# Sums of squares of nine norms: four blocks added on VectorE, four multiplications with ones in place of eight

## The chip, the cores and the metric

The kernel runs on one core of one Trainium2 chip. The metric is the device time of one execution in microseconds (us), the median of several runs. A core has four engines that compute, each with an instruction queue of its own worked off in order: TensorE (PE in the profile; PEld is its loading of weights), VectorE (DVE), ScalarE (ACT) and GpSimd (POOL). The queue of SyncE (SP) issues the DMAs. Engines wait for one another by semaphores.

## The reference

Two transformer-like blocks of two layers each, all in float32, on 256 tokens of width 1024. The first block has a gated recurrence, an mLSTM and an attention to a memory in each layer, merged, projected and added to the stream x, then a dense feed-forward (layer 0) or eight experts (layer 1). The second block has two streams, x and a context, with differential, neighbourhood and windowed attention and feed-forwards modulated by a condition vector. Ahead of each part stands a root-mean-square norm over the 1024 values of a token:

```python
def rms_norm(x, g):
    xf = x.astype(jnp.float32)
    y = xf * lax.rsqrt(jnp.mean(xf * xf, axis=-1, keepdims=True) + EPS)
    return (y * g.astype(jnp.float32)).astype(x.dtype)

        x = x + merged @ w_out[l]
        h2 = rms_norm(x, norm_ffn_g[l])
        ...
        x = x + f
    return rms_norm(x, final_norm_g)
```

The change concerns the norms whose input is just being made by a projection with a residual, as `h2` here.

## The kernel before

**Layout.** The stream x lies transposed in SBUF, as eight blocks of 128 features by 256 tokens. A product in float32 is made from three products of rounded halves: each weight tile (128 x 2048 values, 1 MB, in one of three slots) is copied to its high half by ScalarE (line 1855, WH) and its low half is subtracted by VectorE (line 2244, WL); TensorE then does high by high, high by low and low by high for each of the blocks summed over (lines 1534 to 1536). A projection of eight 128-row blocks takes 24 matmuls for each output block of 128 features; a weight tile serves two output blocks. The last slices of the feed-forwards have fewer rows to sum over: 18 matmuls a block in g0c, g0x and g1 (tiles of 128 x 1536).

**The residual and the norm.** When TensorE has an output block in PSUM, VectorE adds it to x (line 2395 in the first part, line 2421, scaled, in the second; `kout`, by pairs of blocks, for x1.1). ScalarE squares the new block of x into a scratch (line 1874, `nsq`). The sum over the features runs across partitions, so TensorE makes it: a 128x128 matrix of ones times each of the eight blocks of squares, accumulated in one PSUM bank (line 1564, `nsum`). Then VectorE scales the mean (line 2295), ScalarE takes the inverse root (line 1880), VectorE refines it (lines 2268 to 2270) and applies it (line 2319), and the halves of the result are made for the next projection (lines 1897, 1902, 2327, 2330).

**The order.** The program is a list of units, written out by a planner that runs when the kernel is built (`Plan`). `put` appends a unit and moves the planner's clock by the cost of TensorE's part; the costs of the other engines are in `work`. Each engine then goes through the list and issues its part of each unit, so an engine's order is that of the list. Chains of attention and the like are threaded between the units of a projection (`weave`) when the clock has passed the time at which their next step is due. A weight tile is split ahead: unit `tile` stands in front of a pair of output blocks, and its split is that of the tile three later in the list.

**The nine norms.** `follow(name)` gives the function that is called behind each output block i of a projection: it appends the squaring of block i and, from i = 1 on, the sum of block i-1; behind block 7 also that of block 7. It serves f0 and f1 (behind `wo`), x1 (behind the last products of `ffn`), c0.1 and x0.1 (behind `wab0` and `wab1`), c1.0, x1.0 and final2 (behind the last slices of `g0c`, `g0x`, `g1`) and x1.1 (behind `wc`, whose pairs of blocks end only in the last quarter of its matmuls). The other norms (x0, mem0, mem1, c0.0, final1, x0.0) are summed in other ways. The bank of the sums is taken with the first sum and held until `root`, the unit `nmid`.

Of the kernel before, what the change touches and what calls it, by code (L numbers as in the profile page):

```python
# [10 lines left out]
F32 = mybir.dt.float32  # L11
# [4 lines left out]
T = 256  # L16
# [224 lines left out]
def work(p, unit):  # L241
# [37 lines left out]
    if kind == "napp":  # L279
        if len(args) > 1:  # L280
            return ((V, 0.85),) if args[1] < 4 else ((A, 0.6), (V, 0.65))
        if p.norms[args[0]]["dst"] is None:
            return ((V, 3.2),)
        return ((V, 6.4), (A, 0.4), (V, 0.8)) if "gn" in p.norms[args[0]] else ((V, 5.2), (A, 0.55), (V, 0.7))
    if kind == "nsq":
        return ((A, 0.33 * (args[2] - args[1])),)
# [10 lines left out]
class Plan:  # L297
# [190 lines left out]
    def follow(self, name):  # L488

        def after(i):  # L490
            self.squares(name, i, i + 1)
            if i:
                self.sums(name, i - 1, i)
            if i == 7:
                self.sums(name, 7, 8)
        return after
# [976 lines left out]
def tensor_program(nc, T_, pe, plan, mem, v):  # L1473
# [92 lines left out]

    def ada(l, q):
# [27 lines left out]
    def s(name, qb, m):  # L1595
# [6 lines left out]
        if spec["bias"]:  # L1602
            pe.wait_ge("band_r")
            if spec["kind"] == "near":
                tile = plan.tile["bias", spec["hd"]]
                pe.wait_ge(f"land{tile.slot}", tile.turn)
                b = tile.raw[:, 0, qb * T:qb * T + T]
            else:
                b = mem["BAND"][:, 128 + qb * T:128 + qb * T + T]
            eight = mem["BAND"][:, 0:128]  # L1610
            last = T_.matmul(ps[:, 256:512], eight.bitcast(F32) if spec["kind"] == "near" else eight, b, start=False, stop=True)
# [208 lines left out]
    do = {"lin": lin, "kout": kout, "nsum": nsum, "ada": ada, "turned": turned, "s": s, "t": t, "v": vv, "sub1": sub1, "rope1": rope1, "if": iff, "acol": acol,  # L1820
# [406 lines left out]
def vector_program(nc, V, dv, plan, mem, v):  # L2227
# [63 lines left out]

    def nmid(name):
        m, y, u = (R[:, i, :] for i in range(3))
        dv.wait_ge("ps", "norm", name, 8)
        V.tensor_scalar(m, bank(("norm", name))[:, 0:T], 1.0 / D, EPS, mult, add).then_inc(*dv.done("norm_m", name))
        dv.frees("norm", name)
        dv.wait_ge("norm_s", name)
        rstd(m, y, u)
# [461 lines left out]
    do = {"start": start, "lam": lam, "tile": tile, "lin": lin, "nmid": nmid, "napp": napp, "cvd": cvd, "turned": turned, "e": e,  # L2760
# [270 lines left out]
```

## Time and profile before

| | |
|---|---|
| median of 3 runs | 3476.21 us (3470.22 to 3481.88) |
| profiled execution | 3476.61 us, span of the trace 3474.8 us |
| TensorE matmuls busy | 3299.8 us, 95% |
| VectorE busy | 2332.3 us, 67% |
| ScalarE busy | 1838.8 us, 53% |
| granted clock of TensorE, mean | 0.971 of full |
| chain that ended last | TensorE 77%, VectorE 12%, ScalarE 8% |

The profile shows one execution. Times are microseconds from the start of the span, durations of groups are means. In a timeline or chain a row is one or several equal instructions: start, duration, engine, line of the kernel, operation, what it writes and reads, their number (x2), and in square brackets how long the engine was idle before it and which engine and line ended that. Matmuls are pipelined and the ends shown are modelled, so the distance between starts is what a matmul costs. `CTX` in the rows of the first part is a scratch of the norm, which shares its place with the context of the second part. The chain of waits is followed back from the last instruction.

### The profile page before, as it was taken

The numbers are of one execution on the slowest core, as the hardware profiler recorded it, in microseconds if no ns is written. First come the engines' busy times: TensorE is split into PE (matmuls) and PEld (weight loads), VectorE is DVE, ScalarE is ACT, GpSimd is POOL, SyncE is SP. The second block draws the span as 40 slices with busy tenths as digits, with TensorE's granted clock in tenths as the row PEclk, the third lists the DMA queues.
The fourth block names the chain that finished last, engine by engine and source line by source line (L and its number), as shares of the span: only waits on it lengthen the run. The fifth ranks groups of instructions, "written<-read, shape, count | busy, mean of one in ns | idle before, by whom it ended". The sixth has DMA issues, their size and how long they took to land.

```text
span 3474.8 us, 56477 instructions
## 1 busy us (share of the span) xinstructions
PE 3299.8 (95%) x24379; PEld 3047.0 (88%) x24379; DVE 2332.3 (67%) x2986; ACT 1838.8 (53%) x2194; POOL 0.2 (0%) x4
## 2 busy tenths in 40 slices
PE   8999999999899899999999999899799999999798
PEld 7988999999889799999999999888587889985698
DVE  6876655578766588888888888745565556465454
ACT  5464544454635377777777777633443444335343
POOL 0000000000000000000000000000000000000000
PEclk9999999999999899999999999999799999999899
DMA  6432565454325599899899899611233456530353
GB/s 249 170 134 97 182 231 194 158 194 146 134 97 184 214 373 351 327 355 350 333 351 352 334 352 344 252 68 61 109 111 134 141 222 233 211 127 13 134 191 112
DMA packets 102815, 723.43 MB, mean 208 GB/s; under 512 B 11680, under 2 KB 13344, under 8 KB 16672
## 3 DMA queue, kind: packets, MB, share of 16 engines
q1 hardware_dynamic: 102560, 719.73, 56.3%
q8 instruction: 196, 3.21, 0.4%
q14 instruction: 59, 0.48, 0.0%
HBM read 718.64 MB, written 1.05 MB: 207 GB/s over the span
## 4 chain that ended last, share of the span: by engine, by line
PE 77%; DVE 12%; ACT 8%; issue 2%; DMA 1%; SPq 0%; DVEq 0%; ACTq 0%
PE PS L1534 13%; PE PS L1535 13%; PE PS L1536 13%; PE PS L1487 6%; PE PS L1485 6%; PE PS L1486 6%; DVE WL L2244 4%; ACT WH L1855 3%; PE PS L1793 3%; PE PS L1791 3%; PE PS L1792 3%; PE PS L1632 2%; PE PS L1601 2%; PE PS L1564 1%; PE PS L1577 1%
## 5 line engine op out<-in xcount | busy, mean ns | idle before, releaser
L2244 DVE TENSOR_TENSOR WL<-RAW,WH 128x2048 fp32r<-128x2048 f32 (+2 forms) x428 | 963.0, 2252 | 578.0 <-ACT WH L1855 572.4
L1855 ACT ACTIVATE WH<-RAW 128x2048 fp32r<-128x2048 f32 (+2 forms) x428 | 802.6, 1878 | 252.7 <-PE PS L1536 183.6
L1534 PE MATMUL PS<-PH,WH 128*128 128x256 f32 x2464 | 710.8, 288 | 39.2 <-DVE PL L2440 7.9
L1536 PE MATMUL PS<-PH,WL 128*128 128x256 f32 x2464 | 697.2, 283 | 0.0
L1535 PE MATMUL PS<-PL,WH 128*128 128x256 f32 x2464 | 697.2, 283 | 0.0
L2244 DVE TENSOR_TENSOR WL<-F,WH 128x2048 fp32r<-128x2048 f32 x210 | 481.2, 2292 | 87.4 <-ACT WH L1855 86.4
L1534 PE MATMUL PS<-HPH,WH 128*128 128x256 f32 (+1 forms) x1648 | 496.7, 301 | 24.6 <-DVE HPL L2330 12.6
L1534 PEld LDWEIGHTS PS<-PH,WH 128*128 128x128 f32 x2464 | 471.2, 191 | 47.9 <-issue 29.2
L1535 PE MATMUL PS<-HPL,WH 128*128 128x256 f32 (+1 forms) x1648 | 481.2, 292 | 0.0
L1536 PE MATMUL PS<-HPH,WL 128*128 128x256 f32 (+1 forms) x1648 | 480.8, 292 | 0.0
L1535 PEld LDWEIGHTS PS<-PL,WH 128*128 128x128 f32 x2464 | 471.1, 191 | 1.3
L1536 PEld LDWEIGHTS PS<-PH,WL 128*128 128x128 f32 x2464 | 471.0, 191 | 0.0
L1855 ACT ACTIVATE WH<-F 128x2048 fp32r<-128x2048 f32 x210 | 402.3, 1916 | 77.8 <-PE PS L1793 48.4
L1485 PE MATMUL PS<-WH,PH 128*128 128x256 f32 x1456 | 420.1, 289 | 2.0 <-ACT PL L2117 1.0
L1486 PE MATMUL PS<-WL,PH 128*128 128x256 f32 x1456 | 410.4, 282 | 0.0
L1487 PE MATMUL PS<-WH,PL 128*128 128x256 f32 x1344 | 379.8, 283 | 0.0
L1534 PEld LDWEIGHTS PS<-HPH,WH 128*128 128x128 f32 x1648 | 318.5, 193 | 42.1 <-issue 23.6
L1535 PEld LDWEIGHTS PS<-HPL,WH 128*128 128x128 f32 x1648 | 319.2, 194 | 4.7
L1536 PEld LDWEIGHTS PS<-HPH,WL 128*128 128x128 f32 x1648 | 318.4, 193 | 4.5
L1485 PEld LDWEIGHTS PS<-WH,PH 128*128 128x128 f32 x1456 | 274.3, 188 | 5.3 <-ACT WH L1855 1.2
L1486 PEld LDWEIGHTS PS<-WL,PH 128*128 128x128 f32 x1456 | 275.8, 189 | 3.0
L1487 PEld LDWEIGHTS PS<-WH,PL 128*128 128x128 f32 x1344 | 253.6, 189 | 0.0
(382 smaller groups left out, 5072.8 us busy)
## 6 DMA issues: line engine op xcount, KB each, us to landing
F<-in_moe_w SPq DMA_DIRECT2D x210, 1024.0 KB, 5.5
RAW<-in_ffn_w SPq DMA_DIRECT2D x130, 1024.0 KB, 4.9
RAW<-in_moe_w SPq DMA_DIRECT2D x126, 1024.0 KB, 5.1
RAW<-in_w_in SPq DMA_DIRECT2D x64, 1024.0 KB, 4.9
F<-in_ada_w SPq DMA_DIRECT2D x18, 1024.0 KB, 11.5
RAW<-in_w_kv SPq DMA_DIRECT2D x16, 1024.0 KB, 4.9
G<-in_ada_w SPq DMA_DIRECT2D x15, 1024.0 KB, 10.4
RAW<-in_w_in_ab SPq DMA_DIRECT2D x12, 1024.0 KB, 5.0
```

Of the source, the lines that this page charges most:

```text
L1485: T_.matmul(out, lh, rh, start=i == 0, stop=False)
L1486: T_.matmul(out, lh, rl, start=False, stop=False)
L1487: last = T_.matmul(out, ll, rh, start=False, stop=i == n - 1)
L1534: T_.matmul(out, lh, rh, start=first, stop=False)
L1535: T_.matmul(out, lh, rl, start=False, stop=False)
L1536: last = T_.matmul(out, ll, rh, start=False, stop=end)
L1601: last = T_.matmul(ps, l, r, start=i == 0, stop=i == len(ops) - 1 and not spec["bias"])
L1791: T_.matmul(out, oh[:, c], wh, start=j == 0 and k == 0, stop=False)
L1792: T_.matmul(out, oh[:, c], wl, start=False, stop=False)
L1793: last = T_.matmul(out, ol[:, c], wh, start=False, stop=j == 13 and k == 1)
L1855: S.activation(mem["WH"][:, t.s % NHL, 0:m], v.raws[t.slot][:, 0:m], ACT.Copy).then_inc(*ac.done("w_hi", t.s))
L2244: V.tensor_tensor(mem["WL"][:, t.s % NHL, 0:m], v.raws[t.slot][:, 0:m], mem["WH"][:, t.s % NHL, 0:m].bitcast(F32), sub).then_inc(*dv.done( ...
```

## The change

Four of the eight sums of squares of each of the nine norms go to VectorE. `follow` still appends the squaring of block i behind block i. Behind blocks 2 to 5 it appends a new unit `nadd` for block i-1: VectorE waits for the square of that block and adds it to the square of block 0, in place. The units `nsum` in mid-projection are gone. Behind block 7, a bank is taken and one unit `nsum2` is appended, with a cost of 1.72 us in the planner: TensorE waits for the four adds and multiplies the added block 0 with ones, then blocks 5, 6 and 7, each with its wait for the square, into one bank. `nadd` costs 0.35 us of VectorE in the planner. In `s` the two cases of the bias matmul are written out apart.

```diff
--- before.py
+++ after.py
@@ -282,6 +282,8 @@
         if p.norms[args[0]]["dst"] is None:
             return ((V, 3.2),)
         return ((V, 6.4), (A, 0.4), (V, 0.8)) if "gn" in p.norms[args[0]] else ((V, 5.2), (A, 0.55), (V, 0.7))
+    if kind == "nadd":
+        return ((V, 0.35),)
     if kind == "nsq":
         return ((A, 0.33 * (args[2] - args[1])),)
     return OTHER.get(kind, ())
@@ -489,10 +491,11 @@
 
         def after(i):
             self.squares(name, i, i + 1)
-            if i:
-                self.sums(name, i - 1, i)
+            if 1 < i < 6:
+                self.put("nadd", name, i - 1)
             if i == 7:
-                self.sums(name, 7, 8)
+                self.bank(("norm", name), self.bgc, True)
+                self.put("nsum2", name, cost=1.72)
         return after
 
     def modulation(self, n, slots=None, after=()):
@@ -1564,6 +1567,16 @@
             last = T_.matmul(PS[:, plan.banks.place["norm", name], 0:T], ones, v.blocks(tmp, k, k + 1)[:, 0, :], start=k == 0, stop=k == 7)
         last.then_inc(*pe.done("ps", "norm", name, k1))
 
+    def nsum2(name):
+        tmp, out = scratch_of(plan, name), bank(("norm", name))[:, 0:T]
+        consts()
+        pe.wait_ge("added", name, 4)
+        T_.matmul(out, ones, v.blocks(tmp, 0, 1)[:, 0, :], start=True, stop=False)
+        for k in (5, 6, 7):
+            pe.wait_ge("sq", name, k)
+            last = T_.matmul(out, ones, v.blocks(tmp, k, k + 1)[:, 0, :], start=False, stop=k == 7)
+        last.then_inc(*pe.done("ps", "norm", name, 8))
+
     def ada(l, q):
 
         c, b = mem["C32"], plan.banks.place["ada", l, q]
@@ -1601,14 +1614,12 @@
             last = T_.matmul(ps, l, r, start=i == 0, stop=i == len(ops) - 1 and not spec["bias"])
         if spec["bias"]:
             pe.wait_ge("band_r")
-            if spec["kind"] == "near":
-                tile = plan.tile["bias", spec["hd"]]
-                pe.wait_ge(f"land{tile.slot}", tile.turn)
-                b = tile.raw[:, 0, qb * T:qb * T + T]
-            else:
-                b = mem["BAND"][:, 128 + qb * T:128 + qb * T + T]
-            eight = mem["BAND"][:, 0:128]
-            last = T_.matmul(ps[:, 256:512], eight.bitcast(F32) if spec["kind"] == "near" else eight, b, start=False, stop=True)
+        if spec["kind"] == "near" and spec["bias"]:
+            tile = plan.tile["bias", spec["hd"]]
+            pe.wait_ge(f"land{tile.slot}", tile.turn)
+            last = T_.matmul(ps[:, 256:512], mem["BAND"][:, 0:128].bitcast(F32), tile.raw[:, 0, qb * T:qb * T + T], start=False, stop=True)
+        elif spec["bias"]:
+            last = T_.matmul(ps[:, 256:512], mem["BAND"][:, 0:128], mem["BAND"][:, 128 + qb * T:128 + qb * T + T], start=False, stop=True)
         last.then_inc(*pe.done("ps", "s", name, qb, m))
 
     def t(name, qb):
@@ -1817,7 +1828,7 @@
             pe.wait_point("region_end", ("act", "dve"))
         pe.leave(had)
         plan.swap()
-    do = {"lin": lin, "kout": kout, "nsum": nsum, "ada": ada, "turned": turned, "s": s, "t": t, "v": vv, "sub1": sub1, "rope1": rope1, "if": iff, "acol": acol,
+    do = {"lin": lin, "kout": kout, "nsum": nsum, "nsum2": nsum2, "ada": ada, "turned": turned, "s": s, "t": t, "v": vv, "sub1": sub1, "rope1": rope1, "if": iff, "acol": acol,
           "ml": ml, "router": router, "rtop": rtop, "slots": slots, "tt": tt, "gather": gather, "up": up, "turn": turn, "down": down,
           "finish": finish, "region": region}
     for kind, *args in plan.units:
@@ -2288,6 +2299,14 @@
         dv.turn(V.tensor_scalar(e, lam, -1.0, 0.0, mult, mx))
         dv.turn(V.tensor_tensor(q, q, e, add))
         V.tensor_scalar(mem["LAMS"][:, :], q, -2.0, None, mult).then_inc(*dv.done("lam"))
+
+    def nadd(name, k):
+        tmp = scratch_of(plan, name)
+        total = v.blocks(tmp, 0, 1)[:, 0, :]
+        dv.wait_ge("sq", name, k)
+        if k > 1:
+            dv.wait_ge("added", name, k - 1)
+        V.tensor_tensor(total, total, v.blocks(tmp, k, k + 1)[:, 0, :], add).then_inc(*dv.done("added", name, k))
 
     def nmid(name):
         m, y, u = (R[:, i, :] for i in range(3))
@@ -2757,7 +2776,7 @@
             last = V.scalar_tensor_tensor(mem["GN"][:, l, i, s_, :], mem["MOD"][:, l, s_, (3 * i + 1) * 8:(3 * i + 2) * 8], 1.0,
                                               P(f"norm_g2_{l}{i}", 0, 8), add, mult)
         last.then_inc(*dv.done("gains", l, i))
-    do = {"start": start, "lam": lam, "tile": tile, "lin": lin, "nmid": nmid, "napp": napp, "cvd": cvd, "turned": turned, "e": e,
+    do = {"start": start, "lam": lam, "tile": tile, "lin": lin, "nadd": nadd, "nmid": nmid, "napp": napp, "cvd": cvd, "turned": turned, "e": e,
           "n": n, "sub2": sub2, "rope2": rope2, "rgc": rgc, "row": row, "acol": acol, "ml": ml, "pair": pair, "yml": yml, "mgd": mgd, "h2d": h2d, "kout": kout,
           "router": router, "rtop": rtop, "slots": slots, "ttl": ttl, "sel": sel, "gather": gather, "up": up, "turn": turn, "leave": leave, "finish": finish,
           "region": region, "second": second, "lam2": lam2, "gains": gains}
```

## Rows read from the trace of the kernel before

**Rows 1.** The page, busy time by engine.

```profile
PE 3299.8 (95%) x24379; PEld 3047.0 (88%) x24379; DVE 2332.3 (67%) x2986; ACT 1838.8 (53%) x2194; POOL 0.2 (0%) x4
```

**Rows 2.** Waits of TensorE: us in total, times, longest us.

```profile
PE PS L1564 <- ACT G L1874: 15.9, 15, 3.0
PE PS L1564 <- ACT CTX L1874: 11.5, 7, 7.9
```

**Rows 3.** Timeline of TensorE, end of final2: start us, us, instruction, count, idle before it.

```profile
3459.68 0.28 PE L1536 MATMUL PS<-HDH,WL 128*128 128x256 f32 x1
...
3460.35 0.28 PE L1535 MATMUL PS<-HDL,WH 128*128 128x256 f32 x1
...
3462.39 0.59 PE L1564 MATMUL PS<-G,CST 128*128 128x256 f32 x2
3463.58 0.70 PE L1564 MATMUL PS<-G,CST 128*128 128x256 f32 x2 [0.60 <-ACT G L1874]
```

**Rows 4.** Timeline of VectorE, end of final2.

```profile
3462.59 0.48 DVE L2421 SCALAR_TENSOR_TENSOR X<-PS,MOD,X 128x256 f32<-128x256 f32 x1 [2.10 <-PE PS L1536]
...
3465.28 0.43 DVE L2268 TENSOR_TENSOR R<-R 128x256 f32<-128x256 f32 x1 [0.55 <-ACT R L1880]
```

**Rows 5.** Timeline of TensorE, first sum of f0.

```profile
448.09 0.67 PE L1564 MATMUL PS<-CTX,CST 128*128 128x256 f32 x2 [0.76 <-ACT CTX L1874]
```

**Rows 6.** Timeline of VectorE, residuals 5 and 7 of f0.

```profile
461.51 0.42 DVE L2395 TENSOR_TENSOR X<-X,PS 128x256 f32<-128x256 f32 x1 [1.23 <-PE PS L1536]
...
468.07 0.42 DVE L2395 TENSOR_TENSOR X<-X,PS 128x256 f32<-128x256 f32 x1 [1.22 <-PE PS L1536]
```

**Rows 7.** Chain of work in c1.0, start us, us, what.

```profile
2789.53 1.91 ACT WH L1855
2791.46 2.29 DVE WL L2244
2793.75 0.41 DVE CTX L2421
2794.18 0.43 ACT G L1874
2794.65 0.70 PE PS L1564 x2
```

**Rows 8.** Timeline of TensorE, sum 6 of x1 and of x0.1.

```profile
724.59 1.13 PE L1564 MATMUL PS<-CTX,CST 128*128 128x256 f32 x4 [0.63 <-ACT CTX L1874]
...
2823.13 1.13 PE L1564 MATMUL PS<-G,CST 128*128 128x256 f32 x4 [1.64 <-ACT G L1874]
```

**Rows 9.** Timeline of VectorE, tail of x0.1 and first residuals of x1.1.

```profile
2817.74 4.49 DVE L2244 TENSOR_TENSOR WL<-RAW,WH 128x2048 fp32r<-128x2048 f32 x2 [2.29 <-ACT WH L1855]
...
3239.65 0.87 DVE L2421 SCALAR_TENSOR_TENSOR X<-PS,MOD,X 128x256 f32<-128x256 f32 x2
```

**Rows 10.** Busy time by stretch: TensorE, its weight loads, VectorE, ScalarE, GpSimd, clock, DMA.

```profile
2489.80:2493.00 3.20, 0.25 (x3) 0.11 (x2) 3.17 (x5) 0.42 (x1) 0.00 (x0) 1.00 0.11 13
2493.20:2497.80 4.60, 4.60 (x27) 4.56 (x26) 2.73 (x8) 1.69 (x2) 0.00 (x0) 0.63 0.53 214
```

**Rows 11.** Chain of work behind the sums of x1.1.

```profile
3252.54 3.59 PE PS L1577 x64
```

**Rows 12.** DMA issues from 3215 to 3262 us: size, median us to landing.

```profile
RAW<-in_ada_w SPq DMA_DIRECT2D x2, 1024.0 KB, 8.8
```

**Rows 13.** Chain of work over the span, the same two places in each layer.

```profile
225.81 7.17 PE PS L1632 x32
...
442.93 1.91 ACT WH L1855
...
916.72 7.17 PE PS L1632 x32
...
1135.43 1.91 ACT WH L1855
```

**Rows 14.** Busy time of an attention stretch, columns as in rows 10.

```profile
2505.00:2777.00 272.00, 252.54 (x1735) 218.60 (x1733) 151.68 (x254) 116.81 (x176) 0.00 (x0) 0.96 0.33 121
```

## The prediction

> **What bounds the kernel now.** I read the shares of the engines first, then the list of TensorE's waits, then the timelines and chains of the nine places that the change touches. TensorE's matmuls fill 95% of the span [rows 1], so work taken from TensorE comes off the time wherever nothing else is late. The sums of the norms (line 1564) are among the longest waits: TensorE stood 15.9 and 11.5 us in front of them for ScalarE's squares, 7.9 us of that once at the start of the program, outside the change [rows 2]. So there are two things to gain, the sums' own matmuls and waits in front of those in mid-projection, and one question: what ends each projection once the sums are gone. That is read from VectorE and ScalarE, which in the same microseconds split the weights of the next tiles, add the residual and square it, in program order.
>
> **What a sum costs.** A sum is two passes of the array (x2). At the end of final2, the last norm, the matmul ahead of a sum starts at 3459.68 and the second matmul behind it at 3460.35 [rows 3]; from there to the next sum at 3462.39 are 17 matmuls, 0.12 us each. 0.67 less two steps of 0.12 is **0.43 us** a sum, with TensorE never idle. In all nine norms that are summed as their projection goes (f0, x1, f1, c0.1, c1.0, x0.1, x1.0, x1.1, final2) sum k stands behind block k+1, so six sums (0 to 5) stand ahead of the end of block 7, the last of the projection: 6 x 0.43 = 2.6 us.
>
> **What the new tail costs.** After block 7 the kernel before does sum 6, waits for the square of block 7 and does sum 7: 3462.39 to 3463.58 from the start of one to that of the other [rows 3], 1.19 us. The new tail has three matmuls there (the added blocks 0 to 4, block 5, block 6), 3 x 0.43 = 1.29 us, so sum 7 starts 0.1 us later. What covers them is the residual, 0.48 [rows 4], the square, 0.43 [rows 7], and the steps between; without that cover they would cost 0.86 us each time.
>
> **What the adds cost.** Four tensor-tensor adds of 128x256 on VectorE for each norm, 36 in all. The nearest row is the same operation and shape at line 2268, 0.43 us [rows 4]; a residual add counts 0.41 to the next start [rows 7]. Each add waits for a square that is a block old. Behind it in VectorE's order stand the next residual, the low half of the next weight tile and, in c0.1, steps of softmax; for those TensorE waits later. Where VectorE idles (1.23 us before the residual at 461.51 [rows 6]) the add is free. Between the residuals of the two blocks that follow a weight split it isn't: there it lies on the loop below. Bounds: 0 and 36 x 0.41 = 14.8 us; I take what each place gives.
>
> **The loop that takes over.** For each pair of blocks ScalarE squares the second block (0.43), copies the high half of a weight tile (1.91), VectorE subtracts for the low half (2.29), and only then adds the residuals of the next two blocks, whose squares follow [rows 7]. Start to start that is 0.43 + 1.93 + 2.29 + 0.43 = 5.1 us, and 0.41 for the second residual: 5.5 before, up to 5.9 with an add between the residuals. TensorE's side is two blocks of 24 matmuls, 6.56 us with two sums (461.51 to 468.07 [rows 6]), 5.7 without; in c1.0 and x1.0, whose projections end with blocks of 18 matmuls, 36 x 0.12 = 4.3 us. So:
>
> - f0 and f1: 5.7 against 5.5 to 5.9, level. Six sums 2.6, plus the wait of 0.76 in front of sum 0 [rows 5], less 0.25 for an add between residuals 4 and 5 and for the tail: **3.1 each, 6.2**.
> - final2 has no more weights to split: 2.6 - 0.1 = **2.5**.
> - x0.1: two tiles are split together behind block 5 (4.49 us) [rows 9], and TensorE already waits 1.64 us in front of sum 6 [rows 8]. Only sums 0 to 3 stand ahead of block 5's end: 4 x 0.43 = **1.7**.
> - x1: it waits 0.63 us in front of sum 6 [rows 8], and VectorE also makes halves of another norm in each block. The loop rules from block 2: sum 0 and a wait of 0.4 in front of it, **0.8**.
> - c1.0 and x1.0: the loop rules already. For c1.0: high half 2789.53, low half 2791.46, residual 2793.75, sum 2794.65 [rows 7]. What is saved before block 3 (two sums and a wait of 0.7, 1.6 us) shrinks to 0.7 at the next split, since residual 3 comes behind residual 2, a half of another product and an add, and to 0.2 at the last, behind one add more: **0.2**; x1.0, without the other product's halves, **0.5**. TensorE ends block 7 some 4 us (c1.0) and 3 us (x1.0) before the last square.
> - c0.1: softmax of attention heads runs between its blocks. The wait of 2.95 us in front of sum 4 (2489.8 to 2493.0, TensorE busy 0.25 of 3.20) goes [rows 10], but VectorE has that softmax behind its weight split, and residuals 5 to 7 move by less than a microsecond: **0.9**; bounds -1 (the adds in front of softmax) and 5.5 (2.6 + 2.95).
> - x1.1: its squares start in the last quarter of its matmuls, 12 a pair of blocks, 1.4 us, and TensorE has idled by then for the residual at 3239.65 [rows 9]; the sums end at 3252.54 [rows 11]. After: VectorE has 0.8 for residuals and 0.8 for adds a pair, so the first pair of residuals ends at 3240.5, the last at 3240.5 + 3 x 0.8 + 4 x 0.4, or 3244.6 with a step of waiting; squares 3245.1, sums 3245.9. That is 6.6; 1.7 goes back to the clock (below): **4.9**. The matmuls behind (line 1577) need two loads that took 8.8 us each [rows 12], the last about when it is wanted; bound -2 if it is late.
>
> Sum: 6.2 + 2.5 + 1.7 + 0.8 + 0.2 + 0.5 + 0.9 + 4.9 = 17.7 us.
>
> **The clock.** Behind the 2.95 us wait the granted clock was 0.63 over 4.60 us [rows 10]: 0.37 x 4.60 = 1.7 us of work lost, part of it at 1.2 GHz instead of 2.4. The new waits in the tails of c1.0 (4 us) and x1.0 (3 us) are as long or longer, so I take 1.7 us each, +3.4; the bounds are 0 and twice that. The Trainium skill (TensorE: Matmul & The Clock Gate, section Loop structure matters more than you think) says that VectorE's work on results between tiles leaves the array warm and that a long wait for a DMA cools it. The row at 2493.2 speaks against that, since no DMA was waited for. By the page the sum would keep its 17.7.
>
> **The order.** The planner in the program counts 1.72 us for the sums at a norm's end where it counted 3.44, and holds a PSUM bank for a shorter time, so its later choices (between which blocks a softmax step is put) may differ. I cost that at nothing, since the engines' totals hardly change, with a bound either side: the same stretch of layer 0 (225.81 to 442.93) and of layer 1 (916.72 to 1135.43), 217.1 and 218.7 us, differ by 1.6 us [rows 13]. Some nine such stretches follow f0 outside the experts' part: 1.6 x 3 = 5 us either way. The experts' part only starts earlier. Lines 1601 to 1611 are rewritten to the same matmuls: nothing.
>
> **Result.** 17.7 - 3.4 = 14.3 us off. The profiled execution took 3476.61 us around a span of 3474.8; 3476.61 - 14.3 = 3462.3, and the median of the runs, 3476.21, lies 0.4 us from it: **3462 us**, -0.4%.
>
> **The rivals.**
> - TensorE bound everywhere: six sums go in nine places (23.2), all waits in front of sums in mid-projection (7.1 of the 19.5 that rows 2 leave, the largest 2.95 [rows 10] and 0.76 twice [rows 5]), 4 more in x1.1 and 1.7 of clock in c0.1: 36.0, 3441 us. For it: 95%. Against: the loop of rows 7 and the waits of rows 8.
> - The clock holds through the tails: 17.7, 3459 us. Against: rows 10; for: those tails may fall otherwise in time. The page above says the same.
> - More clock and a worse order: the tails of x1 and x0.1 (2 us idle) fall to half clock too, 3.4, and order takes 5: 3471 us. For it: their waits come near those that cost the clock.
> - The sums don't come off the path, or the adds eat what they free: 3476 us. Against: 0.67 against 0.24 in rows 3.
> - Slower: in the attention stretches, where softmax is threaded between blocks, TensorE already idles, 272 - 252.5 = 19.5 us in one of them [rows 14]. If the new order puts a weight split (1.91 + 2.29 = 4.2 us [rows 7]) ahead of a softmax step that TensorE waits for, each such place costs 4.2 us. From six of them on (25 us against 14.3 + 10.4) the kernel is slower by more than 0.3%; seven give 3492 us. Against: the two layers' 1.6 us.
>
> **How the numbers follow.** Forecast 0.42, clock holds 0.13, TensorE bound 0.12, clock and order 0.23, no effect 0.04, slower 0.06. About 0.3% (10.4 us) is what a measurement of this kernel can tell from no change. Faster by more: 0.42 + 0.13 + 0.12, less 0.04 for the edge of the forecast: 0.63. Within: 0.04 + 0.23 + 0.04 = 0.31. Slower: 0.06. The range reaches from near the TensorE-bound case, as far as c0.1's bound (4.6 more), order (5) and the clock (3.4) carry it together with 3 of the runs' spread, to past the clock-and-order case: 3446 to 3474.
>
> **What would show it.** 36 adds of 0.4 us on VectorE at the new line; 72 passes in place of 144 for these norms. TensorE's idle time in front of the last sums: 3 to 4 us in c1.0 and x1.0, under 0.3 in f0, f1 and final2. The stretch from x1.1's last quarter to line 1577 shorter by 5 to 7 us. Half clock just behind c1.0 and x1.0. The prediction is wrong if the tails of c1.0 and x1.0 show no wait (then 3441 is near), or if the attention stretches change by more than 5 us.

## The result, and the profile after

The changed kernel takes 3435.8 us (median, 3432.9 to 3442.3), the kernel before 3473.2 us in the same runs: a ratio of 0.9893, 95% interval 0.9871 to 0.9914. That is 37 us off, where 14 were forecast, and below the forecast range of 3446 to 3474 us. The profiled execution took 3434.04 us around a span of 3432.3. One execution of the run e8 below took 10974.8 us at a mean granted clock of 0.283 and is left out of its median.

The page of the changed kernel: busy time by engine. It answers to [rows 1]: 72 matmuls fewer, 36 instructions more on VectorE.

```profile
PE 3272.1 (95%) x24307; PEld 3027.7 (88%) x24307; DVE 2342.6 (68%) x3022; ACT 1844.5 (54%) x2198; POOL 0.2 (0%) x4
```

TensorE's waits in the changed kernel (us in total, times, longest), and one of the two groups of adds from the list of groups (count, us busy, mean ns, idle before). They answer to [rows 2]. Line 1567 is the other norms' sums, which the change doesn't touch. Of the 27.4 us of [rows 2] the waits that began before 7.88, 2237.07 and 2261.10 us (7.88, 1.93 and 0.92 us) stood in front of those other norms. So the nine norms' waits go from 16.7 to 10.1 + 2.4 + 1.8 = 14.3 us: fewer, and now at the ends.

```profile
PE PS L1577 <- ACT G L1885: 10.1, 5, 3.7
...
PE PS L1567 <- ACT CTX L1885: 7.8, 1, 7.8
...
PE PS L1577 <- ACT CTX L1885: 2.4, 1, 2.4
PE PS L1567 <- ACT G L1885: 2.1, 1, 2.1
PE PS L1574 <- DVE G L2309: 1.8, 1, 1.8
...
L2309 DVE TENSOR_TENSOR G<-G 128x256 f32<-128x256 f32 x24 | 10.0, 417 | 0.2
```

The tails in the changed kernel, from the timeline of TensorE (start us, us, instruction, count, idle before): line 1574 multiplies the added block, 1577 blocks 5 to 7. In this order f0, x1, c1.0 (three rows), x0.1, x1.0, x1.1, final2.

```profile
465.46 1.03 PE L1577 MATMUL PS<-CTX,CST 128*128 128x256 f32 x4
...
720.19 1.13 PE L1577 MATMUL PS<-CTX,CST 128*128 128x256 f32 x4 [2.39 <-ACT CTX L1885]
...
2760.60 0.59 PE L1574 MATMUL PS<-G,CST 128*128 128x256 f32 x2
2761.03 0.59 PE L1577 MATMUL PS<-G,CST 128*128 128x256 f32 x2
2765.36 2.07 PE L1577 MATMUL PS<-G,CST 128*128 128x256 f32 x4 [3.73 <-ACT G L1885]
...
2794.18 1.13 PE L1577 MATMUL PS<-G,CST 128*128 128x256 f32 x4 [1.64 <-ACT G L1885]
...
3014.22 1.13 PE L1577 MATMUL PS<-G,CST 128*128 128x256 f32 x4 [2.92 <-ACT G L1885]
...
3210.36 0.72 PE L1574 MATMUL PS<-G,CST 128*128 128x256 f32 x2 [1.80 <-DVE G L2309]
...
3419.83 0.59 PE L1574 MATMUL PS<-G,CST 128*128 128x256 f32 x2
```

No idle time at f0 and final2, 3.7 us at c1.0, 2.9 at x1.0: these are the tails that the prediction described.

**Where the 42.5 us between the two spans lie.** The medians differ by 37.4 us, the two profiled executions by 5 us more. The same work must stand between two cuts. ScalarE copies 638 weight tiles to their high halves in both kernels, in the same order (line 1855 before, 1866 after), so I cut each trace at the starts of these splits, counted from 0:

| splits | what lies there | before us | after us | change |
|---|---|---|---|---|
| 60 to 64 | f0 | 34.18 | 30.36 | -3.8 |
| 100 to 113 | x1 | 67.80 | 67.06 | -0.7 |
| 166 to 169 | f1 | 34.19 | 30.60 | -3.6 |
| 519 to 546 | c0.1 and the heads of differential and neighbourhood attention | 263.18 | 243.81 | -19.4 |
| 546 to 562 | c1.0, x0.1 | 122.67 | 122.08 | -0.6 |
| 562 to 595 | g0x, x1.0 | 190.95 | 190.27 | -0.7 |
| 595 to 604 | windowed attention | 172.30 | 168.91 | -3.4 |
| 604 to 609 | x1.1 | 70.48 | 64.33 | -6.2 |
| 637 to the end | final2 | 27.08 | 24.20 | -2.9 |

The rest of the span gives 1.3 us. One row stands out: 19.4 us in a stretch for which I had 0.9 and "nothing, 5 us either way". Busy time in that stretch, before and after (columns as in rows 10):

```profile
2469.53:2732.71 263.18, 237.82 (x1549) 200.51 (x1548) 147.23 (x263) 113.50 (x179) 0.00 (x0) 0.94 0.32 116
```

```profile
2460.03:2703.84 243.81, 229.19 (x1539) 193.76 (x1538) 148.20 (x267) 118.46 (x183) 0.00 (x0) 0.97 0.35 126
```

TensorE's idle time falls from 25.4 to 14.6 us. Its busy time falls by 8.6 us. Eight matmuls of c0.1's sums are gone, 8 x 0.21 = 1.7 us; the rest is the clock, 0.94 before and 0.97 after.

The planner's lists of units show what else changed. Every unit but sums and adds stands in the same order in both kernels, except between split 520 and the middle of the stretch. There the steps of two attention heads, which went in pairs, go one by one. In the lists below s is a head's scores, e its maximum and exponential, n its scaling, t its transposes, v its product with the values, sub0 to sub2 its own norm; nmid and napp are root and application of c0.1; `...` marks what is left out.

```
before:  t d1.0 0, t d1.1 0 | wab0 block 3, first half | s d1.0 1, s d1.1 1 | second half ...
after:   t d1.0 0 | wab0 block 3, first half | s d1.0 1, t d1.1 0 | second half | e d1.0 1, s d1.1 1 ...

before, behind block 7:  gains, v d1.0, v d1.1, nmid, sub0 d1.0, sub0 d1.1, sub1 d1.0, sub1 d1.1,
                         sub2 d1.0, s d1.2 0, sub2 d1.1, e d1.2 0, s d1.3 0, napp
after, behind block 7:   v d1.0, gains, t d1.1 1, sub0 d1.0, nmid, v d1.1, sub1 d1.0, sub0 d1.1,
                         sub2 d1.0, s d1.2 0, sub1 d1.1, e d1.2 0, napp, sub2 d1.1, s d1.3 0
```

### The profile page after: what moved, and what is told of

Its sections match the earlier page's. It is cut to its first block, busy times and chain, and to the rows that moved or that the text cites. A ratio compares the mean times of both kernels' runs of the same rounds, so it can differ in the third digit from the quotient of the medians.

```text
span 3432.3 us, 56399 instructions
## 1 busy us (share of the span) xinstructions
PE 3272.1 (95%) x24307; PEld 3027.7 (88%) x24307; DVE 2342.6 (68%) x3022; ACT 1844.5 (54%) x2198; POOL 0.2 (0%) x4
## 4 chain that ended last, share of the span: by engine, by line
PE 76%; DVE 12%; ACT 8%; issue 2%; DMA 2%; SPq 0%; DVEq 0%; ACTq 0%
PE PS L1537 13%; PE PS L1539 13%; PE PS L1538 13%; PE PS L1490 6%; PE PS L1488 6%; PE PS L1489 6%; DVE WL L2255 4%; ACT WH L1866 4%; PE PS L1804 3%; PE PS L1802 3%; PE PS L1803 3%; PE PS L1643 2%; PE PS L1614 2%; PE PS L1631 1%; PE PS L1788 1%
```

## The experiments

All have the changed kernel's sums and adds unless said otherwise, and their edits are shown against it. "Old order" is that of the kernel before, "new order" that of the changed kernel. Medians of each run beside those of the kernel before in the same runs:

| run | median us | before us | ratio, 95% interval | splits 519 to 546, us |
|---|---|---|---|---|
| changed kernel | 3435.8 | 3473.2 | 0.9893 (0.9871 to 0.9914) | 243.8 |
| e1 new sums, old order | 3451.4 | 3471.0 | 0.9947 (0.9930 to 0.9963) | 259.3 |
| e5 old sums, new order | 3460.4 | 3473.2 | 0.9966 (0.9954 to 0.9979) | 246.2 |
| e3 third order | 3440.8 | 3471.0 | 0.9916 (0.9900 to 0.9933) | 250.9 |
| e7 other order behind c0.1 | 3449.0 | 3474.2 | 0.9931 (0.9915 to 0.9948) | 256.2 |
| e8 old order behind c0.1's sums | 3440.9 | 3474.2 | 0.9907 (0.9887 to 0.9926) | 250.2 |
| e11 old order, root first | 3451.8 | 3472.7 | 0.9942 (0.9926 to 0.9959) | 258.0 |
| e12 new order, root first | 3430.3 | 3472.7 | 0.9886 (0.9868 to 0.9904) | 241.1 |
| e9 every add twice | 3435.7 | 3474.2 | 0.9894 (0.9878 to 0.9911) | 245.9 |
| e10 eight sums at the end | 3440.8 | 3474.2 | 0.9910 (0.9893 to 0.9927) | 246.7 |
| e6 c1.0's tail moved | 3437.5 | 3473.2 | 0.9896 (0.9876 to 0.9916) | 244.8 |
| e4 five tails moved | 3425.4 | 3471.0 | 0.9867 (0.9850 to 0.9883) | 243.7 |
| e13 root and three tails | 3426.3 | 3472.7 | 0.9872 (0.9853 to 0.9892) | 243.1 |

**e1: the sums without the order.**

```diff
             if i:
+                if i == 1:
+                    self.bank(("norm", name), self.bgc, True)
+                self.clock += 0.43
             if 1 < i < 6:
-                self.put("nadd", name, i - 1)
+                self.units.append(("nadd", name, i - 1))
             if i == 7:
-                self.bank(("norm", name), self.bgc, True)
-                self.put("nsum2", name, cost=1.72)
+                self.clock += 0.43
+                self.units.append(("nsum2", name))
```

> The new sums and adds are issued where the changed kernel issues them, but the planner books their time and their PSUM bank as before, so every other unit of the program stands in the order of the kernel before. Theory A (the part missing from my sum comes from the attention steps' order behind c0.1): only the terms of the norms remain, as the two traces show them, f0 3.8, x1 1.1, f1 3.5, x0.1 1.8, x1.0 0.7, x1.1 5.7, final2 2.8, less 1.7 of clock behind c1.0, 17.7 us, and up to 3 for c0.1: 3452 to 3456 us beside 3473, and the stretch from 2505 to 2777 keeps its 272 us. Theory B (the sums and waits that left c0.1 and TensorE do it all, the order is worth nothing): 3436 us, as the changed kernel.

3451.4 us, 19.5 below the kernel before, half a microsecond under theory A's range; the stretch 519 to 546 took 259.3 us. Theory A, then. The sums by themselves are worth 19.5 us where 14.3 were forecast (17.7 less 3.4 of clock), and c0.1's part of that is 263.2 - 259.3 = 3.9 at most. That part isn't a wait that went: TensorE's idle time in the stretch is 27.4 us in e1 and was 25.4; its busy time is 6.0 us shorter, 1.7 of it the sums' own passes and the rest the clock, 0.96 for 0.94.

**e5: the order without the sums.** The eight multiplications stand where they stood; a bank is held in the place of the new one and the planner's clock is moved as in the changed kernel. The edit is shown against the kernel before; the lines that give the stand-in bank back and take it out of TensorE's waits are left out. A first version without the latter lines, e2, gave no result.

```diff
             if i:
-                self.sums(name, i - 1, i)
+                if i == 1:
+                    self.bank(("norm", name), self.fgc, True)
+                self.units.append(("nsum", name, i - 1, i))
+            if 1 < i < 6:
+                self.busy[V] += 0.35
             if i == 7:
-                self.sums(name, 7, 8)
+                self.units.append(("nsum", name, 7, 8))
+                self.bank(("spare", name), self.bgc, True)
+                self.clock += 1.72
```

> Eight multiplications with ones for each norm in their old places, no adds, but the planner books time and bank as in the changed kernel, so that all other units stand in its order. The new sums in the old order took 3451.4 us beside 3471.0 (-19.5). Theory A: the rest of the changed kernel's 37 us comes from the order of the attention steps and is found here alone: 3451 to 3457 us, and the stretch behind c0.1 is shorter by some 13 us. Theory B: the two only work together (the freed time in c0.1 lets the heads go ahead): 3465 to 3473 us.

3460.4 us, 12.8 below before: a smaller gain than theory A expected and a larger one than theory B. The stretch settles it: busy time from split 519 to 546 in this run,

```profile
2471.70:2717.86 246.16, 230.85 (x1549) 194.84 (x1548) 147.17 (x263) 118.35 (x183) 0.00 (x0) 0.97 0.34 124
```

The same 1549 matmuls as before take 17.0 us less: 10.1 us less idle (15.3 for 25.4), and 7.0 us less busy, which with equal matmuls is the clock. Sums alone give -3.9 in this stretch, order alone -17.0, both -19.4: they nearly add up. By the medians the two runs give 19.5 + 12.8 = 32.3 of the 37.4 us, which the intervals of the three ratios allow. Outside the stretch this trace of e5 was 2.2 us behind the kernel before at split 519, though the units ahead of it stand in the same order, and lost 2.6 in the windowed attention (below). Only c0.1's booking matters: written out with the old booking in one norm at a time, the planner's list changes for c0.1 and for no other.

**What the order changes at c0.1's end.** TensorE's waits from split 519 to 546 in e1, then in the changed kernel (us in total, times, longest):

```profile
PE PS L1541 <- DVE HPL L2353: 5.5, 1, 5.5
PE PS L1655 <- ACT TMP L2027: 3.4, 3, 2.6
PE PS L1581 <- ACT G L1889: 3.4, 2, 2.8
PE PS L1541 <- DVE HPL L2433: 3.1, 2, 1.9
```

```profile
PE PS L1614 <- ACT PQ L1999: 3.6, 2, 2.7
...
PE PS L1614 <- ACT PQ L2010: 1.9, 1, 1.9
PE PS L1577 <- ACT G L1885: 1.8, 2, 1.3
PE PS L1537 <- DVE HPL L2349: 1.3, 1, 1.3
```

The timeline of TensorE in e1 behind the sum (1581), and that of ScalarE:

```profile
2494.26 1.22 PE L1581 MATMUL PS<-G,CST 128*128 128x256 f32 x2 [0.58 <-ACT G L1889]
2495.28 4.82 PE L1647 MATMUL PS<-PQ,G 128*128 128x256 f32 x16
2502.70 1.10 PE L1655 MATMUL PS<-TMP,CST 128*128 128x256 f32 x4 [2.60 <-ACT TMP L2027]
...
2513.49 0.55 PE L1541 MATMUL PS<-HPH,WH 128*128 128x256 f32 x1 [5.54 <-DVE HPL L2353]
```

```profile
2498.41 0.38 ACT L2020 ACTIVATE G<-PS 128x256 f32<-128x256 f32 x1 [4.20 <-PE PS L1647]
2500.14 0.38 ACT L2020 ACTIVATE G<-PS 128x256 f32<-128x256 f32 x1 [1.34 <-PE PS L1647]
2500.54 1.28 ACT L1895 ACT_TABLE_LOAD   x1
2501.83 0.42 ACT L1895 ACTIVATE R<-R 128x256 f32<-128x256 f32 x1
```

Both heads have their product with the values at once (16 matmuls of line 1647), then both wait at once for their own norms on ScalarE and VectorE, the root of c0.1 stands behind both, and TensorE runs out of work twice, 2.60 and 5.54 us. In the new order one head still has transposes and its product to do while the other's norm is worked on. From the last sum to the first matmul of g0ca0 it is 2494.26 to 2513.49, 19.2 us, in e1, and in the changed kernel 2487.20 to 2502.96, 15.8 us. The Trainium skill (PSUM — Partial Sum Buffer, section Engine vs sequencer instructions) says that the queues of ScalarE and VectorE are strictly first in, first out. The rows agree: the root's input was ready at 2495.9, and its table load began at 2500.54, behind a copy that waited 4.20 us.

**e11 and e12: is it the root's place?** One unit moved, in the old order and in the new.

```diff
+        self.units.remove(("nmid", "c0.1"))
+        self.units.insert(self.units.index(("nsum2", "c0.1")) + 1, ("nmid", "c0.1"))
         self.units = splits_ahead(self.units, self.tiles, self.tile)
```

> The run with the sums alone (old order, 3451.4 us), with one unit moved: the root of c0.1 (scaling by VectorE, root by ScalarE, refinement by VectorE) stands directly behind its sum instead of behind the last products of the two heads. In that run the scaling was done at 2495.9 and ScalarE took the root at 2501.8, behind two copies that waited for 16 matmuls of the heads; TensorE then stood 5.5 us for the applied norm. Theory G (the order of the head steps is worth its 12 us because the norm's steps queue between them on ScalarE and VectorE): the table load of 1.3 us and the refinement of 1.4 us leave that queue, about 3 us less in the stretch 519 to 526, 3448 us. Rival (the heads' own steps rule, the norm follows them in any case): no change of that stretch of 83.7 us beyond 0.5.

> The changed kernel with the same unit moved. There the scaling ended at 2488.8, the root was taken at 2494.0 behind one product of the heads, and TensorE stood 2.65 and 1.27 us ahead of g0ca0. Theory G: 2 to 3 us less in the stretch of 70.8 us, 3433 us. Rival: 70.8 within 0.5, 3436 us.

In the old order splits 519 to 526 took 82.4 us for 83.7, and the wait of 5.5 us in front of g0ca0 was still there: 5.53. In the new order they took 68.1 for 70.8, and the median was 3430.3; the intervals of these two runs and of the runs without the move overlap, so the stretches carry this. So the root's place is worth 1.3 and 2.6 us, as part of the cause, but with the root moved in both, the two orders still differ by 258.0 - 241.1 = 16.9 us from split 519 to 546. Theory G holds for the new order and falls short in the old one. That the rest comes from two heads waiting at the same time is what the rows above suggest; no run shows it by itself.

**e3, e7, e8: other orders.** e3 books the bank with block 1 and the time with block 7. e7 adds the first line below, e8 the second:

```diff
     p.apply("c0.1")
     p.gap(3.0)
+    p.clock += 1.72
```

```diff
+    p.clock += -3
     p.lin_all(wab0, p.follow("c0.1"))
```

> The changed kernel's sums and adds, but the bank of the sums is booked with block 1 and the time with block 7, which gives a third order of the attention steps. Theory A (order moves the time by tens of us and has nothing to do with the sums): somewhere between 3436 and 3460 us, not at 3436, with the difference inside 2455 to 2680. Theory B: 3436 within 3 us.

> The changed kernel's sums, adds and order up to the place where the norm c0.1 is applied; 1.72 us are booked back there, so that the attention steps behind it fall into yet another order. In the runs so far the changed kernel's order gained 12 us from the first split of wab0's last tiles to the second split of the g0c part and 5 us in the hundred behind. Theory D (the gain comes from how many head steps are left to feed TensorE while c0.1 is summed, rooted and applied): the first 12 us stay and only the part behind moves, 3432 to 3446 us. Rival (each order is a lottery over the whole stretch): 3446 to 3460 us, the first part changed too.

> The changed kernel's sums and adds with the planner's clock set back 3 us ahead of c0.1's projection: its first blocks come in another order, everything from block 3 on stands in the order of the kernel before. Theory D: the waits at c0.1's end come back as in the run with the sums alone, 3449 to 3455 us. Rival (what counts is where the projection's first blocks stand): 3436 to 3445 us.

e8's expectation misdescribes its edit. By the planner's list the head steps go one by one from block 2 of wab0 to block 7, in places of their own, and only from the gains behind c0.1's last square on does the list stand in the old order. The run took 76.1 us for splits 519 to 526 where e1 took 83.7, and had the waits at c0.1's end as expected (2.60 and 5.35 us): with the heads out of step in the projection's blocks and in pairs behind them, 7.6 us are gained. By its median of 3440.9 us it falls into the rival's range. Theory D was right on the waits and wrong to put the whole gain there. The changed kernel's 70.8 us up to split 526 can't be set beside these two, since more of the heads' work stands behind that split there (371 matmuls ahead of it, 400 in e1, 394 in e8); of its gain on e1, 9.2 us are idle time of TensorE (10.3 for 19.5).

e3, 250.9 us in the stretch, shows that going one by one isn't enough. There too the heads' steps are apart, further than in the changed kernel: the product of the first head stands in block 7, and c0.1's root behind the product of the second. TensorE waits 5.36 and 5.64 us, and is idle 16.6 us from split 519 to 526:

```profile
2502.13 1.19 PE L1652 MATMUL PS<-TMP,CST 128*128 128x256 f32 x2 [5.36 <-ACT TMP L2024]
...
2514.01 2.07 PE L1615 MATMUL PS<-G 64*128 64x512 f32 x2 [5.64 <-ACT PQ L2011]
```

e7 kept the first part, whose units stand in the changed kernel's order (71.9 us, the changed kernel 70.8), but lost 11 us behind it: 256.2 us, and 3449.0. There my slower rival stands in the trace. Waits of TensorE from 2534 to 2719 us in e7, and ScalarE and VectorE ahead of the first of them:

```profile
PE PS L1632 <- DVE PQ L2492: 17.3, 2, 9.3
```

```profile
2594.47 1.91 ACT L1867 ACTIVATE WH<-RAW 128x2048 fp32r<-128x2048 f32 x1 [10.71 <-DMA RAW<-in_ffn_w]
2599.53 0.69 ACT L2000 ACTIVATE PQ<-PS,SM 128x512 f32<-128x512 f32 x1 [3.15 <-DVE SM L2479]
```

```profile
2596.41 2.29 DVE L2256 TENSOR_TENSOR WL<-RAW,WH 128x2048 fp32r<-128x2048 f32 x1 [11.24 <-ACT WH L1867]
2598.62 0.68 DVE L2475 TENSOR_REDUCE SM<-PS 128x1 f32<-128x512 f32 x1
```

A weight split stands ahead of the softmax steps of a head on both engines, the tile's load lands late, and both engines idle 11 us, while TensorE waits 9.33 us for what its transposes read (and 7.93 us in a second place, for the same line of VectorE). I had priced that place at the split's own 4.2 us; with a late load ahead of it, it cost twice that.

Five orders of the same units with the new sums (e1, e7, e3, e8, the changed kernel) thus took 259.3, 256.2, 250.9, 250.2 and 243.8 us in this stretch: the old order is the slowest of them, the changed kernel's the fastest.

**e9 and e10: the adds and the passes by themselves.** e9 adds a second addition behind each of the 36; e10 has no adds, and TensorE multiplies all eight blocks behind block 7; the planner books the same time as in the changed kernel.

```diff
         V.tensor_tensor(total, total, v.blocks(tmp, k, k + 1)[:, 0, :], add).then_inc(*dv.done("added", name, k))
+        again = v.blocks(tmp, k, k + 1)[:, 0, :]
+        V.tensor_tensor(again, again, again, add).then_inc(*dv.done("again", name, k))
```

```diff
-        pe.wait_ge("added", name, 4)
-        T_.matmul(out, ones, v.blocks(tmp, 0, 1)[:, 0, :], start=True, stop=False)
-        for k in (5, 6, 7):
+        for k in range(8):
```

> The changed kernel with a second addition of the same shape behind each of the 36 (its result is used nowhere): 36 x 0.41 = 14.8 us more on VectorE. Theory E (an add is on the path only in x1.1, 4 x 0.41 = 1.6, and between residuals where a weight split rules, 0.4 in some places): 1 to 5 us more, 3437 to 3441 us. Rival (VectorE is on the path at every add): 12 us more, 3448 us.

> The changed kernel without adds: TensorE multiplies all eight blocks of squares with ones behind block 7, in the changed kernel's order. Four passes of 0.43 us more at each of nine ends, 15.5 us of TensorE. Theory F (where TensorE waits for the last square anyway, c1.0, x1.0, x1, x0.1, they cost nothing; at f0, f1, final2, x1.1 they cost 1.7 each, less the adds that leave VectorE, 1.6 in x1.1 and 0.3 in f0 and f1): 4 to 6 us more, 3440 to 3442 us. Rival (all of it is on the path): 3451 us.

e9: 3435.7 us, the changed kernel's own time, with VectorE busy 2354.5 us for 2342.6. The adds cost nothing that the median can show, not even in x1.1 (splits 604 to 609: 64.6 us for 64.3). They aren't free everywhere: in c1.0 and x1.0, where VectorE is on the path, the last waits grow from 3.73 to 3.95 and from 2.92 to 3.59 us, and splits 546 to 557 take 63.1 us for 62.4. e10: 3440.8, 5 us more as theory F had it, though the intervals of the two kernels overlap. The stretches show the sum of it: f0 32.3 us for 30.4, f1 32.3 for 30.6, final2 25.7 for 24.2, and less than the changed kernel in c1.0 (61.7 for 62.4) and x1.0 (189.0 for 190.3). There the extra passes fill the wait (idle time from split 562 to 595: 0.8 us for 3.2) and the granted clock stayed at 1.00 behind both.

**e6, e4, e13: the tails.** Each moves the four multiplications behind work that doesn't need the norm; shown are c1.0 (e6, e4) and x1.0 (e4, e13).

```diff
+    p.late.append([2, lambda: p.tail("c1.0")])
     for t in range(4):
         p.lin(wab, t, x, 2 if t == 2 else NHL)
...
+    p.early(first[0:1])
+    p.tail("x1.0")
     p.root("x1.0")
-    p.early(first[0:2])
+    p.early(first[1:2])
```

> The changed kernel, with the four multiplications moved behind work that doesn't need the norm: c1.0's behind the second block of the next projection, x1's behind the first block of kvK1, x1.0's behind two blocks of cv, x0.1's and x1.1's behind one product of the modulation. TensorE stood idle there 3.7, 2.4, 2.9, 1.6 and 1.8 us, and 1.7 us of clock went behind c1.0. Theory C (these waits and the clock are a cost of the new tails): 5 to 14 us less than the changed kernel, 3422 to 3431 us, full clock behind c1.0. Rival (the engines that made TensorE wait, ScalarE and VectorE, only make it wait further on): 3436 within 3 us.

> The changed kernel with only c1.0's four multiplications moved behind the second block of the next projection. Theory C: the idle 3.7 us and the 1.7 us of clock behind it are a cost of this tail: 3430 to 3432 us where the changed kernel has 3436, and full clock over the stretch that had half. Rival: the weight split that is late behind c1.0 makes TensorE wait one block later: 3434 to 3437 us, the clock at half a few us later.

> The changed kernel with that unit moved and the three tails that may have gained in the run with five moved (x1 behind the first block of kvK1, x0.1 behind a product of the modulation, x1.0 behind two blocks of cv); c1.0 and x1.1 stay, since c1.0 alone gave 3437 us. Expected from the traces: x1.0 2.5 (idle 3.2 to 0.3 in the stretch behind x0.1), x0.1 1, x1 1, the root 2 to 3: 3427 to 3430 us. Rival (ScalarE and VectorE make TensorE wait further on): 3434 to 3437 us.

e6, 3437.5 us: no gain. TensorE in e6, the first matmul of the next projection and the sums (1578) two blocks on:

```profile
2771.06 0.58 PE L1541 MATMUL PS<-HPH,WH 128*128 128x256 f32 x1 [3.06 <-DVE HPL L2643]
...
2778.38 0.59 PE L1578 MATMUL PS<-G,CST 128*128 128x256 f32 x2
```

The projection wab1 needs halves that VectorE makes right behind the same weight split and residual. The wait has only moved to it, the clock fell in e6 and in e4 all the same, and both traces, e6 and the changed kernel, keep their distance of 5.8 us from before c1.0 to behind it. For c1.0 the rival is right. e4 and e13 did gain, 9 to 10 us below the changed kernel (the intervals of e4 and of the changed kernel overlap between 0.9871 and 0.9883, so the stretches carry this): splits 105 to 113 behind x1 took 49.0 us in both for 50.9 to 51.6 in the other traces with the new sums, splits 562 to 595 with x1.0 187.7 and 188.0 for 189.0 to 191.0, idle 0.3 us for 3.2. So the tails of x1 and x1.0 cost 2 us each that a better place gives back, x0.1's about 0.5, c1.0's and x1.1's nothing. e4 and e13 are the fastest versions of this case.

## Why the prediction was wrong where it was

**The bound and the cost of a sum: right.** f0, f1 and final2 were to give 3.1, 3.1 and 2.5 us and gave 3.8, 3.6 and 2.9. 72 passes went, 36 adds of 0.42 us came, and e9 shows those off the path but for some tenths in c1.0 and x1.0, where the prediction had them on it as well.

**The loop that takes over: right.** c1.0 0.2 us and x1.0 0.5 were forecast; splits 546 to 557, with c1.0, took 62.4 us for 62.8, and x1.0's stretch is 0.7 shorter. From the last sum of c1.0 to that of x0.1 it was 28.2 us before and is 28.1: that fits the 1.7 us of x0.1 and the 1.7 of clock that were forecast there and cancel. x1 gave 1.2 for 0.8, of which its tail returned 0.4 in the changed kernel and 1.1 in e1. x1.1 gave 6.2 for 6.6 less the clock; its adds cost nothing (e9), so the mechanism stands and the term was 1.3 short. The 1.7 us that were to go back to the clock there didn't: its mean was 0.85 before and 0.87 after.

**c0.1's own term: mis-sized, within its bounds.** 0.9 with bounds -1 to 5.5; e1 against before gives 3.9 in the whole stretch, the changed kernel against e5 2.4. The reason given, that the wait of 2.95 us in front of sum 4 goes, isn't what e1 shows: one of 2.81 us in front of later sums came for it, and the gain is passes and clock.

**The clock: half right.** Behind c1.0's wait the granted clock was at its lower level of 1.2 GHz, as forecast; behind x1.0's it wasn't in this trace. Busy time by stretch in the changed kernel, columns as in rows 10: c1.0's tail, then x1.0's wait and what follows it.

```profile
2763.80:2770.60 6.80, 5.24 (x20) 4.83 (x21) 4.92 (x7) 3.25 (x5) 0.00 (x0) 0.50 0.41 135
...
3011.00:3014.20 3.20, 0.30 (x2) 0.00 (x0) 3.08 (x3) 0.45 (x2) 0.00 (x0) 1.00 0.27 115
3014.20:3021.00 6.80, 6.78 (x53) 6.64 (x54) 4.33 (x6) 3.87 (x4) 0.00 (x0) 1.00 0.45 157
```

The page of the Trainium skill that the prediction named (TensorE: Matmul & The Clock Gate, section Loop structure matters more than you think) has VectorE's work between tiles leave the array warm. The changed kernel's c1.0 speaks against it, its x1.0 for it: the same kind of wait for VectorE and ScalarE, 3.73 and 2.92 us. Over the traces with these waits the clock fell behind c1.0's every time, for 3.4 or 6.8 us; behind x1.0's it fell in e3, e6, e9 and e11 and held in the changed kernel, e1, e7, e8 and e12. Behind x1's, 2.4 us (2.1 in e11), it fell in e1, e6, e7, e8, e9 and e11 and held in the changed kernel, e3 and e12. Where it fell for 3.4 us at half rate, 1.7 us of work are lost. So behind the shorter waits the same code met either clock, and the chance of it was to be forecast, not a fixed price.

**The order: this is the step that failed.** It said that later choices of the planner may differ and costed that "at nothing", 5 us either way, from the 1.6 us by which two layers differ in the same stretch [rows 13]. e5 shows 17.0 us for the order alone, 10 of them idle time and 7 clock. Of the 28.2 us by which the spans fell further than 14.3, 18.5 lie in this one stretch, 5.0 in the other eight norms with their clock, and 4.7 in work that the change doesn't touch, 3.4 of them in the windowed attention. The prediction's own sign of being wrong, an attention stretch that changes by more than 5 us, came. Both premises of the zero failed. The two layers of [rows 13] run nearly the same order by the planner's list, so their difference measured how one order repeats, not what another order does. And "the engines' totals hardly change" is true (VectorE 147.2 and 147.2 us in the stretch, ScalarE 113.5 and 118.4, the difference being eight table loads of 1.28 us for four) and says nothing: TensorE idled 25 us there in the old order and 15 in the new. The number was in front of me: [rows 14] shows 19.5 us of idle time in this stretch, and I used it for the slower rival alone. An order that costs 4.2 us in a place can as well stop costing it. The bound for the order should have been that idle time and the lost clock, on both sides.

**The rivals.** TensorE bound everywhere gave 3441, near the result, but by another sum: its 36.0 us were to come in nine places, and outside c0.1's stretch those places came to 18.4. Its agreement is luck. The clock holding through the tails (3459) came true for one of the two, x1.0's. The case of more clock and a worse order (3471) had the order's sign wrong, though its clock loss behind x1's tail is there in six traces. The slower rival's mechanism exists (e7), with 8 to 9 us a place instead of 4.2; e7 is still 25 us faster than the kernel before.

**What stays open.** 3.4 us in the windowed attention (splits 595 to 604) with units in the same order. Over fourteen traces it took 167.5 to 174.9 us, the clock making most of it. The 3.4 us lie between splits 602 and 604, 62.1 us at a mean clock of 0.92 before and 58.7 at 0.97 after. The largest difference to another trace is ahead of that: busy time from split 595 to 602 before, after, and in e5 with the old sums.

```profile
3046.33:3156.52 110.19, 107.27 (x705) 83.77 (x703) 67.85 (x165) 46.20 (x94) 0.00 (x0) 0.97 0.24 89
```

```profile
3016.19:3126.43 110.24, 107.33 (x705) 83.91 (x704) 67.84 (x165) 46.20 (x93) 0.00 (x0) 0.97 0.25 91
```

```profile
3030.70:3146.61 115.91, 114.20 (x712) 88.94 (x711) 68.12 (x165) 46.31 (x94) 0.00 (x0) 0.91 0.23 85
```

Why the clock was 0.91 in one and 0.97 in the others is not known: e5 idled less there than both, 1.7 us for 2.9. Open too is which of the moved steps gives the new order its gain: e3 also goes one by one and keeps waits of over 5 us. No run put the heads of other stretches out of step.

## What to carry to other kernels

Where a planner interleaves chains by a model of time, a change in booked cost is a change of order, and it can outweigh the edit: bound it by the idle time and the lost clock of the stretch, on both sides, and measure it alone by issuing the new work under the old booking and the old work under the new. Two chains that take turns on the same engines are worth trying out of step, so that one has matrix work while the other is in its softmax or norm; by how far is to be measured, since one step apart gained here and further apart (e3) brought waits back. Part of a reduction can be left to another engine and its rest to the tail. Such a tail cost nothing at some norms and 2 us at two, and before moving it, look whether the next matmul needs the same late engine.

## What the runs showed of the hardware that was not expected

- TensorE ran at two slightly different rates at full granted clock. In a stretch without any idle time the same 100 us hold 845 matmuls in some executions and 855 in others, 118.7 and 117.3 ns from start to start. Splits 609 to 637 took 158.6 us in seven traces (before and after among them) and 156.85 us in the seven others, never anything between. The changed kernel, then e9:

```profile
3300.00:3400.00 100.00, 100.00 (x845) 100.00 (x844) 54.76 (x55) 40.87 (x40) 0.00 (x0) 1.00 0.52 179
```

```profile
3300.00:3400.00 100.00, 100.00 (x855) 100.00 (x854) 55.48 (x55) 40.91 (x40) 0.00 (x0) 1.00 0.52 183
```

- The same code scatters by 5 us from trace to trace: e6 has the changed kernel's code up to c1.0 and was 5.8 us later there. Spans of single traces can't be compared to better than that. Stretches between equal cuts can where TensorE sets the pace: f0 took 30.36 to 30.63 us in the eleven traces with the new sums and adds, and the two rates above are the exception.
